# A two-block transformer kernel on one core: norms, transposes and stores by token tile, and a reordered recurrent block

## The reference

```python
# first block (norm_mix, norm_mlp gains; norm_final after both layers)
h = h + chunked_band_attention(rmsnorm(h))        # 16 heads
h = h + sq_relu_mlp(rmsnorm(h))                   # relu(x @ w1)**2 @ w2, width 4096
h = h + rglru_block(rmsnorm(h))
h = h + sq_relu_mlp(rmsnorm(h))
# the recurrent block
u = hn @ w_in + b_in; x_br, y_br = u[:, :D], gelu(u[:, D:])
xc = conv_b + sum(shift(x_br, 3 - tap) * conv_w[tap] for tap in range(4))
r, ig = sigmoid(xc @ w_ga + b_ga), sigmoid(xc @ w_gx + b_gx)   # 8 blocks of 128
log_a = -8 * r * softplus(-a_param)
h_t = exp(log_a) * h_{t-1} + sqrt(1 - exp(2 * log_a)) * (ig * xc)
out = (h_t * y_br) @ w_o + b_o
# second block, i = 0: rwkv7 time mix, i = 1: differential attention with its own keys/values
y = mix_i(...)                                   # ends in @ w_out (out_a, out_b)
h = h + rms_norm(y, norm_post[i])
e = p[i] @ ple_w[i]; g = sigmoid(h @ ple_gate[i])
h = h + rms_norm(g * e, ple_norm[i])
# layer 1 begins with k, v = rms_norm(h, kv_norm) @ kv_w and q, gate = rms_norm(h, norm_pre[1]) @ w_in
```

## Time and profile before

| | |
|---|---|
| median of 3 runs | 1199.31 us (1197.18 to 1202.8) |
| profiled execution | 1200.37 us, span 1198.6 us |
| TensorE busy | 1075.3 us, 90% |
| ScalarE, VectorE, GpSimd busy | 535.0, 486.0, 706.1 us |
| granted TensorE clock, mean | 0.952 of full speed |
| loads | 292 pieces of 512 KB, 167.03 MB read |

### The profile page before, as it was taken

The page is one execution under the profiler, slowest core; times in us unless marked ns, Lnnn a source line. Parts: engine busy times, 40 slices in busy tenths (PEclk is TensorE's granted clock), DMA queues, the critical chain, the costliest instruction groups (busy, mean ns, idle before and its releaser), DMA issues. The chain is left out here.

```text
span 1198.6 us, 19877 instructions
## 1 busy us (share of the span) xinstructions
PE 1075.3 (90%) x8416; PEld 883.7 (74%) x8416; DVE 486.0 (41%) x654; ACT 535.0 (45%) x834; POOL 706.1 (59%) x443
## 2 busy tenths in 40 slices
PE   5999999999977699999988999898898869989685
PEld 4788898998877689999964445798846557767554
DVE  1124274352366725321247266435641451223232
ACT  5537374444436755444421151222223564559352
POOL 6956459988837579989830025300035849667660
PEclk8999999999988899999998999899999979999798
DMA  9642345555634345555572343000036425423140
GB/s 367 235 141 71 133 152 190 191 184 189 193 115 151 123 155 180 192 184 187 191 228 88 114 149 123 20 4 3 4 123 223 159 89 192 133 96 123 62 157 36
DMA packets 45848, 169.37 MB, mean 141 GB/s; under 512 B 5088, under 2 KB 5344, under 8 KB 45440
## 3 DMA queue, kind: packets, MB, share of 16 engines
q1 hardware_dynamic: 43312, 159.06, 39.8%
q0 software_dynamic: 2448, 9.05, 2.4%
HBM read 167.03 MB, written 1.05 MB: 140 GB/s over the span
## 5 line engine op out<-in xcount | busy, mean ns | idle before, releaser
L692 POOL TENSOR_TENSOR ring_r<-ring,high_r 128x512 fp32r<-128x512 f32 (+1 forms) x368 | 635.0, 1755 | 263.5 <-ACT high_r L846 262.2
L846 ACT CAST high_r<-ring 128x1024 fp32r<-128x1024 f32 x248 | 256.5, 1048 | 245.8 <-DMA ring<-w 243.5
L424 PE MATMUL psum<-x_high,high_r 128*128 128x256 f32 x640 | 182.6, 285 | 1.6 <-DVE x_low L282 1.6
L424 PE MATMUL psum<-x_low,high_r 128*128 128x256 f32 x640 | 181.5, 284 | 0.0
L424 PE MATMUL psum<-x_high,ring_r 128*128 128x256 f32 x640 | 181.4, 283 | 0.0
L398 PE MATMUL psum<-high_r,x_high 128*128 128x512 f32 x320 | 131.4, 411 | 13.1 <-DVE x_low L278 9.4
L398 PE MATMUL psum<-ring_r,x_high 128*128 128x512 f32 x320 | 128.7, 402 | 0.0
L398 PE MATMUL psum<-high_r,x_low 128*128 128x512 f32 x320 | 128.7, 402 | 0.0
L600 DVE TENSOR_TENSOR arena<-arena 128x512 f32<-128x512 f32 x32 | 51.7, 1616 | 183.5 <-ACT arena L576 183.4
L424 PEld LDWEIGHTS psum<-x_high,high_r 128*128 128x128 f32 x640 | 123.2, 192 | 2.9 <-issue 1.3
L424 PEld LDWEIGHTS psum<-x_low,high_r 128*128 128x128 f32 x640 | 123.2, 192 | 0.6
(11 more groups left out here) (309 smaller groups left out, 1616.6 us busy)
## 6 DMA issues: line engine op xcount, KB each, us to landing
ring<-w SPq DMA_DIRECT2D x292, 512.0 KB, 3.4
row<-rows POOLq DMA_DIRECT2D x14, 512.0 KB, 8.4
arena<-relt SPq DMA_DIRECT2D x2, 1536.0 KB, 14.8
h<-x SPq DMA_DIRECT2D x1, 1024.0 KB, 5.1
arena<-lora POOLq DMA_DIRECT2D x2, 512.0 KB, 6.2
out<-h SPq DMA_DIRECT2D x1, 1024.0 KB, 4.0
con<-consts SPq DMA_DIRECT2D x1, 529.0 KB, 5.5
arena<-pT POOLq DMA_DIRECT2D x2, 256.0 KB, 4.0
```

Source lines behind the costliest of these rows:

```text
L424: ins = nc.tensor.matmul(out, a, b, start=(k == 0 and q == 0), stop=(k == KT - 1 and q == 2))
L692: ins = nc.gpsimd.tensor_tensor(low(m)[:, part], raw(m)[:, part], read(high(m))[:, part], ALU.subtract)
L846: nc.scalar.copy(high(m), raw(m)).then_inc(high_made, 1)
```

## The change

It does several things at once.

1. In both MLPs a semaphore `w2_tile0` is raised when token tile 0's last matmul is done, and VectorE adds tile 0 on it.
2. Recurrent block. The pieces of x, gates and y lie in the order `REC`. TensorE goes x0 to x5, gate step 0, x6, x7, gate step 1, y0, y1, gate steps 2 and 3, y2 to y7. ScalarE adds the x bias and does the last tap with Identity (scale conv_w3, bias cb); VectorE does three taps. The sigmoids become Tanh of half the argument, with constants halved in the decays. The first half's decays come before gate groups 2 and 3. og, its high and its low part go by quarters in place of halves. GpSimd waits for `scan_done` 2 after the last y piece, makes two lows, and waits for the last og part before it goes on. b_o is added after the og parts.
3. `scale_shift(0)` is cut in `rescale(0)` and `weight_bias(0)` and stands after `first_state(1)` and `next_state(1, 1)`.
4. Output, gate and first key and query products: the second output tile, both gate tiles and the first two tiles of W_KVQG go by passes of one token tile (`pe_pass`); a tile's pieces are freed in its second pass. Norm sums, roots, adds to h, transposes (`pe_transpose_slots`, one token tile and four features to a bank) and the gate's elementwise work go by token tile. The embedding product stays in PSUM and is read there by VectorE; the gate goes to banks 4 to 7. Pieces 2 and 3 of W_PLE0 and W_PLE1, which repeat the first two, are loaded with 8 columns each.
5. h is stored in two DMAs, one for each token tile.

```diff
+REC = ["x0", "x1", "x2", "x3", "x4", "x5", "g0", "x6", "x7", "g1", "y0", "y1", "g2", "g3", "y2", "y3", "y4", "y5", "y6", "y7"]
+UNUSED_PIECES = {4 * n + i for n in (W_PLE0, W_PLE1) for i in (2, 3)}
...
-            used_piece(dve, w2_piece(m, 7, 3))
             for t in range(NT):
+                if t == 0:
+                    dve.wait_ge(w2_tile0, m + 1)
+                else:
+                    used_piece(dve, w2_piece(m, 7, 3))
...
+        def pe_pass(pe, n, t, bank, lhs, first=False, last=False, ready=None):
+            for i in range(4):
+                m = 4 * n + i
+                if first:
+                    piece_ready(pe, m)
+                if ready is not None:
+                    ready(i)
+                for j in range(2):
+                    k = 2 * i + j
+                    for q, (a, b) in enumerate(parts([x_[:, k, token_cols(t)] for x_ in lhs],
+                                                     (high(m, 2, HALF)[:, j, :], low(m, 2, HALF)[:, j, :]))):
+                        ins = nc.tensor.matmul(psum[:, bank, :], a, b, start=(k == 0 and q == 0), stop=(k == KT - 1 and q == 2))
+                if last:
+                    ins.then_inc(piece_used, 1)
+            return ins
...
+            low_until(4 * W_RO)
+            pool.wait_ge(scan_done, 2)
+            low_until(4 * W_RO + 2)
+            pool.wait_ge(og_low, 4)
             low_until(4 * W_RKVG)
...
+            split_until(REC_AT["x0"] + RING)
+            conv_start(0)
+            conv_start(1)
+            conv_start(2)
+            act.wait_ge(decay_ready, 1)
+            gates_out(0)
+            conv_start(3)
+            gates_out(1)
+            act.wait_ge(gates_read, 2)
+            decays_of(0)
+            gates_out(2)
+            gates_out(3)
+            act.wait_ge(gates_read, 4)
+            decays_of(1)
...
+            def out_norm(first, e_n, gates):
+                e = 2 * e_n
+                split_for(first)
+                used(act, first)
+                square_half(pair_out(0)[:, 0], 0, 0, e)
+                act.wait_ge(part_gain, 4 * e_n + 1)
+                square_half(pair_out(0)[:, 1], 0, 1, e)
+                split_until(4 * first + 8)
+                act.wait_ge(out_pass, e_n + 1)
+                square_half(pair_out(1)[:, 0], 1, 0, e)
+                token_root(e, 0)
+                split_until(4 * gates + 2)
+                used(act, first + 1)
+                square_half(pair_out(1)[:, 1], 1, 1, e)
+
+            def embed(tile, e_n, T, ahead):
+                e, gates = 2 * e_n + 1, tile + 1
+                evacuate_slot_high(act, T, 0, XH)
+                token_root(2 * e_n, 1)
+                evacuate_slot_high(act, T, 1, XH)
+                split_until(4 * gates + 4)
...
+                act.wait_ge(gate_pass, 2 * e_n + 1)
+                gate_out(0, 0)
+                evacuate_slot_high(act, T, 2, XH)
+                evacuate_slot_high(act, T, 3, XH)
+                split_until(4 * gates + 8)
+                gate_square(0, 0)
+                used(act, gates)
+                gate_out(0, 1)
+                gate_square(0, 1)
+                split_until(ahead - 1)
+                act.wait_ge(gate_pass, 2 * e_n + 2)
+                gate_out(1, 0)
+                gate_square(1, 0)
+                token_root(e, 0)
+                split_until(ahead)
+                used(act, gates + 1)
+                gate_out(1, 1)
+                gate_square(1, 1)
+                token_root(e, 1)
...
             first_state(1)
-            for g in (1, 2):
-                next_state(1, g)
+            rescale(0)
+            next_state(1, 1)
+            weight_bias(0)
+            next_state(1, 2)
...
             def embed_pe(tile, e_n, T):
 
                 pe.wait_ge(lor_landed, 48 + 16 * e_n)
+                for t in range(NT):
+                    pe.wait_ge(h_token, 4 * e_n + t + 1)
+                    pe_transpose_slots(pe, T, h, t)
                     for k in range(2):
-                        m = 4 * tile + 2 * c + k
+                        m = 4 * tile + k
+                        if t == 0:
+                            piece_ready(pe, m)
+                        for c in range(2):
+                            ins = nc.tensor.matmul(psum[:, 2 * c + t, :], pT_sb[:, k, token_cols(t)],
                                                    raw(m)[:, c * HALF:(c + 1) * HALF], start=(k == 0), stop=(k == 1))
-                        ins.then_inc(piece_used, 1)
+                        if t == 1:
+                            ins.then_inc(piece_used, 1 if k == 0 else 3)
+                    if t == 0:
+                        ins.then_inc(e_done, 1)
+                    gate = pe_pass(pe, tile + 1, t, 4 + 2 * t, xT2, first=t == 0, last=t == 1,
+                                   ready=lambda i: bank_out(pe, 4 * T + 2 * t + i // 2))
+                    if t == 0:
+                        gate.then_inc(gate_pass, 1)
+                pe_pass(pe, tile + 2, 0, 5, xT2, first=True).then_inc(gate_pass, 1)
+                pe_pass(pe, tile + 2, 1, 7, xT2, last=True)
...
+            pe.wait_ge(h_token, 3)
+            pe_transpose_slots(pe, T_H7, h, 0)
+            pe_pass(pe, W_KVQG, 0, KVQG_BANK[0], xTb2, first=True, ready=xb_slot(0))
+            pe.wait_ge(h_token, 4)
+            pe_transpose_slots(pe, T_H7, h, 1)
+            pe_pass(pe, W_KVQG + 1, 0, KVQG_BANK[1], xT2, first=True, ready=x_slot(0))
+            pe_pass(pe, W_KVQG, 1, KVQG_BANK[0] + 1, xTb2, last=True, ready=xb_slot(1))
+            pe_pass(pe, W_KVQG + 1, 1, KVQG_BANK[1] + 1, xT2, last=True, ready=x_slot(1))
```

More of the change, by code:

```diff
@@ new lines, in _, with two_inputs @@
+            evacuate_high(act, T_YA, (XH, None))
+            out_norm(W_OUT_A, 0, W_PLE0 + 1)
+            embed(W_PLE0, 0, T_H6, 4 * W_KVQG + 5)
+            def two_inputs(t):
+                for dst, gain, done in ((XBH, c8("kv_norm"), xb_high), (XH, c8("norm_pre1"), tp_act)):
+                    for q in range(2):
+                        g = 4 * T_H7 + 2 * t + q
+                        act.wait_ge(tp_filled, g + 1)
+                        if dst is XH:
+                            act.wait_ge(xb_low, 2 * t + q + 1)
+                        for j in range(4):
+                            k = 4 * q + j
+                            ins = nc.scalar.activation(dst[:, k, token_cols(t)], filled_slot(g)[:, j, :], ACT.Copy,
+                                                       scale=gain[:, k:k + 1])
+                        ins.then_inc(done, 1)
+                    if t == 0 and dst is XBH:
+                        split_until(4 * W_KVQG + 8)
@@ L1567, in add_normed, with token_add @@
+            def token_add(e, t):
+                dve.wait_ge(n_root, 2 * e + t + 1)
+                if e > 0:
+                    dve.wait_ge(h_token, 2 * e + t - 1)
+                cs = norm_cols(e, t)
+                settle(nc.vector.reciprocal(rstd[:, cs], root[:, cs]))
                 for c in range(2):
                     hl = slice(c * HALF, (c + 1) * HALF)
-                    for t in range(NT):
-                        ins = nc.vector.scalar_tensor_tensor(out=h[:, t, hl], in0=posted[:, t, hl],
-                                                             scalar=rstd[:, 2 * i + t:2 * i + t + 1], in1=h[:, t, hl],
-                                                             op0=ALU.mult, op1=ALU.add)
@@ L2053, in _, with out_product @@
                 gate_piece(n // 4, n % 4)
+            def out_product(first, e_n, ready, free=None):
+                pe_chunk(pe, first, 0, xT2, None, ready)
+                if free is not None:
+                    free()
+                pe_pass(pe, first + 1, 0, 2, xT2, first=True).then_inc(out_pass, 1)
+                pe_pass(pe, first + 1, 1, 3, xT2, last=True)
             def embed_pe(tile, e_n, T):
                 pe.wait_ge(lor_landed, 48 + 16 * e_n)
-                pe.wait_ge(part_sq, 8 * e_n + 4)
```

435 lines of the change are left out of this document (250 added, 185 removed).

## The result

The changed kernel takes 1189.19 us, median of six runs (1188.35 to 1193.9), against 1198.78 us for six runs of the kernel before. The ratio is 0.9927, 95% interval 0.991 to 0.9944: 0.7% or 8.8 us faster, where 25.4 us were forecast. The direction was right; 1189 lies above the range of 1163 to 1187. The profiled execution took 1193.9 us, the slowest of the six, with a span of 1191.5.

What follows compares the result with a forecast made beforehand. TensorE bounds the kernel, busy 1075.3 of 1198.6 us, so time moves with its waits and lower clock. Terms -2.7 - 11.8 - 3.4 - 3.7 - 3.8 = -25.4 from the median 1199.3 give 1174 us, range 1163 to 1187.

Steps and rivals of the forecast that it cites:

- parts 1 and 3: Ends of both MLPs and the last state step, forecast 2.7 + 3.4 = 6.1 us faster.
- parts 4 and 5: First and last output and gate products, with the first key products, worked by token tile: forecast -7.5 us.
- 1. End of both MLPs: Token tile 0's adds start 1.36 us before the end of each MLP, shortening both waits: -2.7 us.
- 2. Recurrent block: A shorter elementwise chain starts the output product at 404.3, with TensorE still waiting 6 us: -11.8 us.
- slow start: After a wait TensorE runs near the 1.2 GHz level for a few matmuls; each such start costs about 1.8 us.
- the new wait: TensorE waiting on GpSimd's held-back lows in the recurrent output product: cost 0, at most 3 us.
- 3. State step: Moving scale_shift(0)'s 4.0 us off VectorE's path removes TensorE's wait before the last state step: -3.4 us, bounds -2 to -3.4.
- 4. First output, gate and key products: Token order starts the key product 7.0 us and third key tile 5.5 us earlier, less 1.8: -3.7 us, bounds +3 to -7.
- signs of being wrong: Casts standing long between tanh groups, passes at half clock throughout, or the third key tile waiting more than 2 us.
- the token order wins nothing: Rival: GpSimd's 2.54 us per piece binds pass 0; first and last products win only 3 us of tail: 1178, chance 0.14.
- The ring's route: Rival: passes hold slots, so refill length L enters in full at five places; slower from L = 12.4 us, chance 0.05.
- L = 9.8: Slot freed to low part ready takes 9.8 us, with a 6.1 us landing, instead of 7.3: 12.5 us lost, 1186.

Runs made afterwards that it cites:

- small_only: The kernel before with only token tile 0's early adds at both MLPs' ends and scale_shift(0) moved behind the first state: 1195.42 us, ratio 0.9971.
- scale_only: The kernel before with only scale_shift(0) moved behind first_state(1), without the MLPs' early adds: 1196.90 us, ratio 0.9986.
- hold_off: The changed kernel without GpSimd's waits on scan_done 2 and og_low 4 in the recurrent block: 1192.50 us, ratio 0.9952 to the kernel before.
- tokens_only: The kernel before with only the token passes, norms, transposes and stores by token tile: 1202.36 us, ratio 1.0027.
- rope_late: The changed kernel with GpSimd's first rope step behind the lows of two more third-key-tile pieces: 1183.12 us, ratio 0.9874 to the kernel before.
- embed_early: The changed kernel with both token tiles' embedding product right behind tile 0's transposes, before its gate pass: 1182.16 us, ratio 0.9870 to the kernel before.
- early_late: The changed kernel with both the edits of embed_early and rope_late: 1173.51 us, ratio 0.9796 to the kernel before.
- no_gate_lows: The changed kernel without low parts for the four gate tiles, high parts multiplied instead (gate values wrong): 1176.96 us, ratio 0.9824 to the kernel before.
- tokens_mended: tokens_only with the edits of embed_early and rope_late: 1184.64 us, ratio 0.9883 to the kernel before.
- early_late_kv: early_late with the first two key and query tiles for both token tiles at once: 1179.10 us, ratio 0.9849 to the kernel before.

## Why the prediction was wrong

**Bound and method.** Right: TensorE's busy time moved by 2.0 us, and the time moved by waits. The ledger by parts, forecast and measured: recurrent block -11.8 and -8.4; parts 1 and 3 -6.1 and -3.5; parts 4 and 5 -7.5 and +3.2. That makes -25.4 and -8.7. The step that failed is 4: it priced the embedding product at half of what it takes, let every refill land after 3.6 us, and put the rope step ahead of the third key tile's lows at almost nothing.

**1. End of both MLPs, -2.7: right.** Both waits fell by 1.36 us, the forecast's own number; timed, the difference of small_only and scale_only is 1.8, which is within their noise, so the waits and not the times bear this out.

**2. Recurrent block, -11.8: mechanism right, size off.** Measured -8.4 (interval -11.6 to -5.0), in the trace 10.0 at the product's start. The chain's terms were nearly right: the section is 66.9 us, forecast 404.3 - 339.2 = 65.1. TensorE had its y tiles done at 395.35 in place of 398, so it still waited 9.87 and not 6. From the product's start to the next transposes it needs 26.7 us (405.22 to 431.95), before 25.8 (416.10 to 441.94): a slow start as before, and 0.25 us for the third piece's lows, the new wait for which I allowed 0 to 3. The term for the scans held: hold_off brings back 6.47 us, and the Trainium skill's rule on the lock between two-SBUF-input operations of VectorE and GpSimd (SBUF — State Buffer, "SBUF: two separate sides") fits these runs too: with GpSimd running, the two adds at 957.78 and 964.09 of the changed kernel take 2.80 and 2.77 us, against 1.42 at the end, where it stands still. Timeline of DVE there:

```profile
957.78 2.80 DVE L1722 SCALAR_TENSOR_TENSOR h<-arena,small,h 128x512 f32<-128x512 f32 x2
...
964.09 2.77 DVE L1722 SCALAR_TENSOR_TENSOR h<-arena,small,h 128x512 f32<-128x512 f32 x2
```

**3. State step, -3.4: over-sized.** The mechanism held, the price did not: 1.3 us in the trace, 1.7 timed, on an interval that takes in none. I took the instructions' whole length as what stood on the path, without asking when the last step's operands would be there. The term read from the earlier trace rows, a wait of 3.36 us put down to VectorE, was not all removable, since VectorE itself would next wait for TensorE.

**4. First output, gate and key products, -3.7: wrong, and the step that decides.** Measured +3.9 us in the changed kernel's first section and +3.0 in tokens_only's. Counted from the output product's start, the forecast falls behind as follows.

- *Gates' end*: forecast 964.6 - 905.5 = 59.1 us, measured 958.8 - 896.35 = 62.5. That is 3.4 late. The embedding takes 3.60 us per token tile (eight rows of plain fp32, 0.45 us each), where I wrote 1.7, about what eight split matmuls take. The true price stood in a row of the kernel before that is not among the prediction's, 7.11 us for both token tiles:

```profile
930.93 7.11 PE L2066 MATMUL psum<-ring,arena 128*128 128x512 f32 x16 [1.84 <-DVE arena L1584]
```

  So tile 1's pass and the slots come 1.9 us later for each token tile. The four embedding slots are freed within 1.8 us, behind the gate pass, and the four pieces land over 6.4 us (casts at 939.49 to 945.87), where I gave each 3.6 us. The last piece of the second gate tile starts 55.4 us after the output product; the forecast had its low ready at 957.8 - 905.5 = 52.3.
- *Key product*: forecast 67.3, measured 71.7, so another 1.0. The adds to h take 2.8 us each beside GpSimd.
- *Third key tile*: forecast 93.0, measured 99.5, so another 2.1. I had named the rope step ahead of the lows and given it almost nothing. TensorE's wait of 3.53 us there is its longest for a low part. GpSimd stood idle 16.00 us ahead of the rope step, because the step's input is the first key tile, whole only after its second pass, in an activation that ScalarE has behind casts that wait for landings; rope_late removes TensorE's wait, and 6.4 us with it.
- *After it*: from the third key tile's start to the end of the section it is 16.1 us, by the forecast 13.1, since the third tile begins at the lower clock (0.50 granted over 995.8 to 1000). That is 3.0 more. I had charged 1.8 us for a slow start, but in the second gate tile, and there it did not come: over 925 to 959 the granted clock was 1.00 in spite of the waits of up to 1.4 us. So another 1.2.

Together 7.7 us, from the forecast's -3.7 to +3.9 within rounding. One of the prediction's own signs of being wrong came: the third key tile waited more than 2 us.

embed_early and rope_late undo the two causes one by one, and early_late both. That these causes are the supply's, as the prediction's text said in words ("the supply eats most of what the token order saves"), is shown by no_gate_lows and by tokens_mended. Of the rivals, "the token order wins nothing" named the mechanism of pass 0, bound by GpSimd's rate, but it left these parts a gain of 3.0 us where they lost 3.2. The ring's route had the places right; its case of L = 9.8, which loses 12.5 us and gives 1186, came nearest in number. The refills of the second gate tile took 3.3 to 7.9 us from free to cast in place of 3.6.

Of the table loads that the order by tokens adds, one was on the path. Timeline of ACT in the changed kernel, ahead of tile 1's last sigmoid:

```profile
958.96 1.28 ACT L1184 ACT_TABLE_LOAD   x1
960.26 0.60 ACT L1184 ACTIVATE arena<-psum 128x512 f32<-128x512 f32 x1
```

The gate's last matmul ends at 958.8 (960.63 less its wait of 1.82), and the sigmoid starts 1.45 us later, behind a cast and this load. At the end of the kernel the same load is over 0.49 us before the matmuls are, and costs nothing. A load is 1.28 us in every row here; the 2.7 us of the Trainium skill (ScalarE: Activation LUTs, "Table sets: the hidden batching unit") no row shows.

**5. Last output and gate products, -3.8: nearly right, by other terms.** The last section is 3.5 us shorter. The tail gives 3.0, as forecast. From the last add to the span's end it is 3.1 us, before 4.5: 1.4 rather than 0.4 for the store. The gates end 0.9 us later in their section than before, where I had 2.2 less 1.8 sooner: the same supply as in part 4.

## What to carry to other kernels

When a tile's work is cut in two passes, its buffer slots live longer; before counting what the earlier start wins, write down when each slot is freed, by which instruction, and which engine's queue the refill must pass. Move the last use of a slot ahead of work that doesn't need it (here one product of 3.6 us, worth 0.6%), and look in each helper's queue for a step that waits for late data in front of steps whose data is there (here one rope step, worth 0.5%). A wait that names an engine as its releaser is worth, when that work is removed, only what is left until the next releaser.

## What the runs showed of the hardware

**The clock after a wait differs between executions and kernels.** Windows of the changed kernel and of the kernel before behind the second MLP (columns as in the earlier trace rows):

```profile
621.60:628.60 7.00, 5.33 (x18) 3.87 (x19) 4.67 (x12) 1.68 (x4) 0.00 (x0) 0.50 0.00 0
```

```profile
633.00:640.00 7.00, 5.37 (x21) 3.65 (x22) 4.67 (x12) 1.68 (x4) 0.00 (x0) 0.77 0.00 0
```

They are the same work behind waits of 8.15 and 9.51 us, one at the 1.2 GHz level throughout, one at a mean of 0.77. Next, tokens_only, early_late and the changed kernel over the attention's first 15 us:

```profile
1021.30:1036.00 14.70, 14.64 (x49) 11.17 (x50) 2.53 (x7) 5.32 (x12) 8.08 (x7) 0.77 0.23 74
```

```profile
999.30:1014.30 15.00, 14.94 (x64) 11.45 (x64) 4.31 (x11) 7.64 (x20) 10.86 (x10) 1.00 0.32 105
```

```profile
1013.80:1028.80 15.00, 14.96 (x64) 11.45 (x64) 4.34 (x11) 7.66 (x20) 7.47 (x7) 1.00 0.32 105
```

All three begin alike, behind a wait of 0.87 or 0.88 us; tokens_only makes 49 matmuls in 14.7 us, the others 64 in 15. The whole attention, from its first transposes to the end of a wait of 8.0 us that every kernel has some 97 us later, shows the price. In eight of the nine kernels without a wait of 3 us or more at the third key tile (the kernel before among them) it is 97.0 to 97.1 us, in early_late_kv 98.7. In the five with that wait it is 98.7 (the change, hold_off, no_gate_lows), 101.5 (embed_early) and 101.6 (tokens_only). The two go together, but the wait is not shown to be the cause. In embed_early, tokens_only, hold_off and early_late_kv the attention's start is slow. In the change and no_gate_lows it is not. Every kernel has two more waits in the attention, of 2.78 us some 34 us on and of about 2.40 us 48 to 50 us on. Over the 8 us behind them the granted clock is 1.00 and 0.79 in the kernel before, 0.79 and 1.00 in rope_late, 0.79 and 0.79 in the change: a second slow stretch, and not the third key tile, goes with its extra 1.6 us. Here is the stretch at the second of them in the change and in rope_late:

```profile
1059.90:1067.90 8.00, 5.95 (x26) 4.87 (x26) 1.75 (x4) 2.49 (x7) 4.57 (x4) 0.79 0.11 44
```

```profile
1051.20:1059.20 8.00, 5.92 (x32) 5.00 (x33) 2.39 (x6) 3.94 (x9) 4.61 (x4) 1.00 0.29 95
```

This accounts for what the sections leave open. In the profiled executions tokens_only loses 3.0 + 4.5 - 3.4 us there and is 0.7 ahead at the first output product, 3.4 in all (3.2 timed); rope_late gains 4.4 + 1.6 of its 6.4 us. Each figure is one profiled execution; what decides which of the waits is followed by a slow stretch is open.

**Four loads started together land one after the other.** In the changed kernel the embedding product of 934.38 frees one slot after its first half, at 936.2, and three at 938.0; the casts of the new pieces begin at 939.49, 942.61, 943.83 and 945.87; a single 512 KB load took 3.6 us from free to landed.
